# Gated linear attention and mLSTM on one core: two of eight score products joined, the weight sum of mLSTM taken from summed tiles, and the gate product split over two groups of rows

## The chip, the cores and the metric

The kernel runs on one core of one Trainium2 chip. The metric is the device time of one execution in microseconds (us): the median of several runs. The engines named below are PE (the matrix engine, with its weight loads shown apart as PEld), DVE (the vector engine), ACT (the scalar engine), POOL (GpSimd) and SP, which issues transfers. SBUF is the on-chip memory with 128 partitions, PSUM the memory that PE writes its products to, in banks of 512 float32 columns.

## The reference, cut to what matters

One layer of a decoder on 512 tokens and 16 meta tokens. Its token mixing has three branches; the change touches two of them, each with four heads.

```python
def gla_chunk_step(S, xs):                 # gated linear attention (GLA)
    q, k, v, g = xs
    G = jnp.cumsum(g, axis=2)
    causal = jnp.tril(jnp.ones((C, C), bool))
    diff = G[:, :, :, None, :] - G[:, :, None, :, :]
    decay = jnp.exp(jnp.where(causal[None, None, :, :, None], diff, -jnp.inf))
    A = jnp.einsum("bhtk,bhtsk,bhsk->bhts", q, decay, k)
    o = jnp.einsum("bhtk,bhkv->bhtv", q * jnp.exp(G), S) + jnp.einsum("bhts,bhsv->bhtv", A, v)
...
    g = jax.nn.log_sigmoid((a_lr @ p["w_gla_a2"] + p["b_gla_a"]).astype(jnp.float32)) / GLA_TAU
...
def mlstm_chunk_step(carry, xs):
    P = jnp.exp(D - m[..., None]) * jnp.einsum("bhtk,bhsk->bhts", q, k)
    num = w_inter[..., None] * jnp.einsum("bhtk,bhkv->bhtv", q, Cs) + jnp.einsum("bhts,bhsv->bhtv", P, v)
    den = w_inter * jnp.einsum("bhtk,bhk->bht", q, ns) + jnp.sum(P, axis=-1)
    h = num / jnp.maximum(jnp.abs(den), jnp.exp(-m))[..., None]
```

## The kernel before, in words

All engines run programs written out by hand, in a fixed order; they wait for each other by semaphores. PE is given one long list of work. Its bulk are the projections (`gemm`), each of them three products of a high and a low part of weights and activations in the type `fp32r`, a shortened float32 (PE's rows print it as `f32` too). Their weights stream in by transfers (`wraw`) and are split by POOL into `whi` and `wlo`, four chunks ahead at most. Results go to two PSUM tiles `GP`, used in turn; the attention work between them uses the four banks of `PA`, called `bank(0)` to `bank(3)`. A product with plain float32 operands is shown in the trace as two records, one behind the other.

**GLA.** Inside a tile of 128 tokens the decay between a query and an earlier key can't be one factor, since it would overflow. So the 128 x 128 weights of a tile are put together from seven levels, `LEVELS = [64, 32, 16, 8, 4, 2, 1]`, and the diagonal. On a level with blocks of B tokens, queries in the odd blocks meet keys in the even block just before. For each level DVE writes the two halves of the exponents into `E` (`lv_write`), ACT takes the exponential (`level`), DVE multiplies the 256 queries into `QL` and the 256 keys into `KL` (`lv_mul`), PE takes four products of 64 columns (`level`, L2129), and DVE copies the wanted entries into `AT` under a mask (`lv_select`, L1451). The diagonal is `level(h, 7)`: the plain product of `kh` and `qh`, four times 128 x 128 (L2132), of which `lv_select` takes the diagonal (L1454). Between the levels PE does pieces of the projections of the next head: level 6 and the diagonal stand between two halves of `gv..A` (L1845; in the last head a gate, L1830). Behind the second half PE waits for the last selection, for `KHt` (L1459) and for `km` (`twice`, L1186), and transposes them (L2183, L2185).

**The gate product.** `gemm("gg..")` (L1850) multiplies the 16 rows of `w_gla_a2`, put into rows 32 to 47 of the otherwise zero `a2`, with `small`, 128 rows of 528 columns, in two halves of 264 columns that go to two banks. Head 0's stands before the level loop, those of heads 1 to 3 between levels 0 and 1 of the head before.

**mLSTM.** For four blocks j of keys, `AT[:, j, :]` holds the weights of all queries from `FROM[j]` on (`FROM = [0, 112, 240, 368]`), so 512, 400, 272 and 144 columns, and `ATt` the 16 last queries' weights for the last 16 keys. `weights_of(h, j)` on DVE makes them from the scores and from `Wd` (ACT, `decay`). PE's `recalled` sums over the blocks in PSUM (L2239, L2240): twice with the values, into banks 0 and 1, and a third time with `ones`, into bank 3, which is the sum of the weights. `denominator` on DVE reads it. DVE's own order behind `weights_of(h, 3)` is: the convolutions of the next head (`conv`, `conv_mul`), with `km` at their end, then `denominator(h)` and `head_sums(h)`, for which PE's `squares` (L2147) in the next head waits.

Of the kernel before, what the change touches and what calls it, by code (L numbers as in the profile page):

```python
# [24 lines left out]
D = 1024  # L25
SEQ = 512
# [265 lines left out]
def build(nc, a, line, scratch, rows, out):  # L292
# [3 lines left out]
    with ctx:  # L296
# [6 lines left out]
        def region(offset, specs):  # L303
# [67 lines left out]
        AO = YO + 2 * KT * SEQ * 4  # L371
        (sgate, gtmp, vb, qh, kh, vh, vm, AT, ATm, sqo, rso, on, km) = region(AO, [
            ("sgate", [P, 2, SEQ], FP32), ("gtmp", [P, 2, SEQ], FP32), ("vb", [P, D], FP32),
            ("qh", [P, 2, SEQ], FP32), ("kh", [P, 2, ALL], FP32), ("vh", [P, 2, QT, DV], FP32),
            ("vm", [P, 2, DV], FP32), ("AT", [P, QT, SEQ], FP32), ("ATm", [P, SEQ], FP32),
            ("sqo", [P, 2, SEQ], FP32), ("rso", [P, SEQ], FP32), ("on", [P, 2, SEQ], FP32), ("km", [P, 2, P], FP32)])
# [7 lines left out]

        (zc, cv, sgc, lf_, bcum_, M_, uT, uTt, fbias_, um_, Mb, Md, Wd, Mt, Wt, ATt, later_t, ones16) = region(BO, [
            ("zc", [P, ALL + 3], FP32), ("cv", [P, ALL], FP32), ("sgc", [P, ALL], FP32), ("lf", [P, ALL], FP32),
# [3 lines left out]
            ("Mt", [2 * META, META], FP32), ("Wt", [2 * META, META], FP32), ("ATt", [P, META], FP32),  # L390
            ("later_t", [2 * META, META], FP32), ("ones16", [P, P], FP32)])
        later = ATm
        states, keysT = AT[:, :, P:P + DV], AT[:, :, P + DV:SEQ]

# [233 lines left out]
        def _(act):  # L628
# [538 lines left out]
        def _(dve):  # L1167
# [201 lines left out]
            dve.wait_ge(gla_c, 1)  # L1369
            dve.wait_ge(ld_a, 32)  # L1370

# [11 lines left out]
            def q_in(h):  # L1383
                ts(qh[:, h % 2, :], ready(f"gq{h}")[:, 0:SEQ], cc("gq", h), DK ** -0.5, ALU.add, ALU.mult).then_inc(gfree[tl[f"gq{h}"].slot], 1)

# [25 lines left out]
            def lv_write(h, l):  # L1411

                B = LEVELS[l]
                lo_, up = parts(G[:, h % 2, META:ALL], B)
                N = SEQ // (2 * B)
                mid = lo_[:, :, B - 1:B].broadcast_to([P, N, B])
                k = len(LEVELS) * h + l
                if k:
                    dve.wait_ge(lv_qk, k)
                dve.wait_ge(G_ok, h + 1)  # L1420
                tt(E[:, 0:SEQ // 2].rearrange("p (n b) -> p n b", b=B), up, mid, ALU.subtract)
                tt(E[:, SEQ // 2:SEQ].rearrange("p (n b) -> p n b", b=B), mid, lo_, ALU.subtract).then_inc(lv_w, 1)

            def lv_mul(h, l):
                B = LEVELS[l]
                k = len(LEVELS) * h + l
                dve.wait_ge(lv_e, k + 1)
                if k >= 2:
                    dve.wait_ge(lv_ps, 8 * ((k - 2) // 7) + (k - 2) % 7 + 1)
                _, uq = parts(qh[:, h % 2, :], B)  # L1430
                lk, _ = parts(kh[:, h % 2, META:ALL], B)
                lo_, _ = parts(KL[:, k % 2, :], B)
                tt(QL[:, k % 2, :].rearrange("p (n b) -> p n b", b=B), uq, E[:, 0:SEQ // 2].rearrange("p (n b) -> p n b", b=B), ALU.mult)
                if k:
                    dve.wait_ge(lv_qk, k)
                tt(lo_, lk, E[:, SEQ // 2:SEQ].rearrange("p (n b) -> p n b", b=B), ALU.mult).then_inc(lv_qk, 1)

            def lv_select(h, l):
                k = 8 * h + l
                dve.wait_ge(lv_ps, k + 1)  # L1440
                if k == 8 * h and h:
                    dve.wait_ge(av_ps, h)
                if k:
                    dve.wait_ge(lv_sel, k)
                if l < len(LEVELS):
                    B = LEVELS[l]
                    n_ = P - B
                    o_ = AT[0:n_, :, 0:P].rearrange("p t (n two b) -> p t n two b", two=2, b=B)[:, :, :, 1, :]
                    m_ = lm[0:n_, l, :].rearrange("p (n b) -> p n b", b=B).unsqueeze(1).broadcast_to([n_, QT, 64 // B, B])
                    d_ = bank(k % 4)[0:n_, 0:QT * 64].rearrange("p (t n b) -> p t n b", t=QT, b=B)  # L1450
                    nc.vector.copy_predicated(o_, m_.bitcast(U32), d_).then_inc(lv_sel, 1)  # L1451
                else:
                    m_ = ident[:, :].unsqueeze(1).broadcast_to([P, QT, P])
                    nc.vector.copy_predicated(AT[:, :, 0:P], m_.bitcast(U32),  # L1454
                                              bank(k % 4).rearrange("p (t n) -> p t n", t=QT)).then_inc(lv_sel, 1)

            def off(h):
# [3 lines left out]
                twice(km[:, h % 2, 0:2 * META], KHt[:, 0:META], km_ok)  # L1461
                tt(QQ[:, :], QQ[:, :], qh[:, h % 2, :], ALU.mult).then_inc(od_q, 1)
                if h + 1 < HEADS:
# [100 lines left out]
            def gate_rows_of(m):  # L1564

                if m == 0:
                    nc.vector.memset(zc[:, 0:3], 0.0).then_inc(zpad, 1)
                    nc.vector.memset(M_[GR, :], 1.0).then_inc(M_one, 1)
                    nc.vector.tensor_copy(bcum, small[96:96 + HEADS, :]).then_inc(ms_d, 1)
# [3 lines left out]
                if m == 1:  # L1573
                    dve.wait_ge(fl_ok, 1)
                    seq(ts(bcum, bcum, 0.0, None, ALU.min))
                    seq(tt(lf, bcum, lf, ALU.subtract))
                    dve.wait_ge(M_one, 1)
                    seq(nc.vector.tensor_tensor_scan(bcum, M, lf, 0.0, ALU.mult, ALU.add))
# [9 lines left out]
                if m == 4:  # L1588
                    nc.vector.memset(ATt[:, :], 0.0)
                    nc.vector.memset(later[:, :], 0.0)  # L1590
                    nc.vector.memset(ones16[:, :], 0.0).then_inc(ml_c, 1)
                    dve.wait_ge(ml_c, 1)
                    nc.vector.memset(ones16[0:META, :], 1.0).then_inc(ml_c, 1)
                if m == 5:
# [57 lines left out]
            def weights_of(h, j):  # L1652
# [29 lines left out]
            for q in range(2):  # L1682
                conv(0, q)
                conv_mul(0, q)
            dve.wait_ge(ml_c, 3)
            dve.wait_ge(ld_v, 16)
            for part in range(3):
                values("mv", 0, part)
            for h in range(HEADS):
# [8 lines left out]
                weights_of(h, 2)  # L1698
                weights_of(h, 3)
                if more:  # L1700
                    conv(h + 1, 0)
# [96 lines left out]
        def _(pe):  # L1798
# [9 lines left out]
            def gemm(name, part=None):  # L1808
# [304 lines left out]

            pe.wait_ge(ld_a, 32)

            def level(h, l):
                k = 8 * h + l
                if l < len(LEVELS):
                    pe.wait_ge(lv_qk, 7 * h + l + 1)
                if k >= 4:  # L2120
                    pe.wait_ge(lv_sel, k - 3)
# [3 lines left out]
                for i in range(QT):  # L2125
                    if l < len(LEVELS):
                        b = (7 * h + l) % 2
# [20 lines left out]

            for nm in ("gq0", "gk0", "gg0", "gv0A", "gv0B", "gv0M"):
                gemm(nm)  # L2150
            for h in range(HEADS):
# [24 lines left out]
                level(h, 6)  # L2176
                level(h, 7)
                nxt("gvA", 1)
# [63 lines left out]
            for h in range(HEADS):  # L2242
# [8 lines left out]
                if h == 0:  # L2251
                    pe.wait_ge(ml_c, 3)
                nxt("mq", 0)
# [145 lines left out]
```

## Time and profile before

| | us |
|---|---|
| median of 3 runs | 1278.88 |
| lowest, highest | 1278.63, 1279.53 |
| the profiled execution, whole | 1279.91 |
| its span, first to last instruction | 1278.2 |
| PE busy in it | 1270.2 |
| DVE, ACT, POOL busy in it | 613.8, 393.9, 774.5 |
| granted TensorE clock | 1.0 throughout |

The trace shows GLA from about 347 to 570 us of the span, mLSTM from about 665 to 800 us. PE is busy for 99% of the span. A merged row of the timeline gives the first start and the busy time of several records of one line. The records of PE overlap, since the modelled end of a matmul includes its way through the array; how long a group holds the engine is therefore read from one start to the next start, not from the busy column.

### The profile page before, as it was taken

Reading aid. Unit: us, or ns where it says so; the run is one execution under the profiler, and the core shown is the slowest. Engines: PE = TensorE matmul, PEld = TensorE weight load, DVE = VectorE, ACT = ScalarE, POOL = GpSimd, SP = SyncE. Lnnn points to the kernel's source line nnn. Section 1 sums busy time; section 2 is a strip of 40 time slices with the busy share of each in tenths; the row PEclk is TensorE's granted clock in tenths of the full one; section 3 lists DMA queues with packets and bytes.
Section 4 is the critical chain, followed back from the end, with each engine's and each line's share of the span. In section 5 each row is a group of like instructions: output and inputs, shape, how many; then the busy total and the mean of one; then the engine's idle time right before and its main releaser. Section 6 shows DMA issues by size and latency. Waiting matters only on the chain.

```text
span 1278.2 us, 17629 instructions
## 1 busy us (share of the span) xinstructions
PE 1270.2 (99%) x6665; PEld 1043.6 (82%) x6668; DVE 613.8 (48%) x1090; ACT 393.9 (31%) x810; POOL 774.5 (61%) x919
## 2 busy tenths in 40 slices
PE   9999999999999999999999999999999999999998
PEld 8866887676899899888898887787888888888886
DVE  4248788652266877825445562242611112333434
ACT  4243565543013324234023333311501101221322
POOL 8737430034763753758774446786677667788882
PEclk9999999999999999999999999999999999999999
DMA  7755200222322312222442323533233333222321
GB/s 186 221 173 166 75 17 26 66 68 79 95 74 60 83 50 67 74 76 83 114 111 72 85 83 99 172 108 99 67 100 98 99 85 113 99 84 98 100 83 66
DMA packets 168444, 120.59 MB, mean 94 GB/s; under 512 B 12393, under 2 KB 146639, under 8 KB 168360
## 3 DMA queue, kind: packets, MB, share of 16 engines
q1 hardware_dynamic: 161654, 108.32, 29.1%
q10 hardware_dynamic: 6706, 11.15, 2.6%
q8 instruction: 53, 0.87, 0.3%
q14 instruction: 31, 0.25, 0.1%
HBM read 115.20 MB, written 9.62 MB: 98 GB/s over the span
## 4 chain that ended last, share of the span: by engine, by line
PE 99%; ACT 0%; DVE 0%; issue 0%; DVEq 0%; ACTq 0%
PE GP L1830 45%; PE GP L1865 9%; PE PA L1865 9%; PE GP L1845 7%; PE GP L1827 7%; PE PA L2029 3%; PE GP L2091 3%; PE PA L2239 2%; PE PA L2129 2%; PE PA L2066 1%; PE GP L2312 1%; PE GP L1910 1%; PE PA L1999 1%; PE PA L2231 1%; PE PA L2030 1%; PE GP L1837 1%
## 5 line engine op out<-in xcount | busy, mean ns | idle before, releaser
L623 POOL TENSOR_TENSOR wlo<-wraw,whi 128x256 fp32r<-128x256 f32 x712 | 565.9, 826 | 14.8
L619 POOL TENSOR_SCALAR whi<-wraw 128x1024 fp32r<-128x1024 f32 x178 | 201.6, 1132 | 464.5 <-PE GP L1830 228.7
L1830 PE MATMUL GP<-xh,whi 128*128 128x512 f32 x352 | 145.5, 413 | 0.0
L1830 PE MATMUL GP<-xh,wlo 128*128 128x512 f32 x352 | 139.1, 395 | 0.0
L1830 PE MATMUL GP<-xl,whi 128*128 128x512 f32 x352 | 138.9, 394 | 0.0
L1772 DVE TENSOR_TENSOR ul<-U,uh 128x512 fp32r<-128x512 f32 x64 | 65.4, 1057 | 109.4 <-ACT uh L1146 109.4
L1830 PE MATMUL GP<-nl,whi 128*128 128x512 f32 x240 | 95.1, 396 | 0.0
L1830 PE MATMUL GP<-nh,wlo 128*128 128x512 f32 x240 | 95.1, 396 | 0.0
L1830 PE MATMUL GP<-nh,whi 128*128 128x512 f32 x240 | 95.1, 396 | 0.0
L1776 DVE SCALAR_TENSOR_TENSOR U<-GP,rrow 128x512 f32<-128x512 f32 x32 | 22.1, 691 | 141.7 <-PE GP L1830 140.3
L1830 PEld LDWEIGHTS GP<-xh,whi 128*128 128x128 f32 x352 | 66.2, 188 | 16.3 <-issue 2.0
L1830 PEld LDWEIGHTS GP<-xh,wlo 128*128 128x128 f32 x352 | 66.1, 188 | 15.3
L1830 PEld LDWEIGHTS GP<-xl,whi 128*128 128x128 f32 x352 | 66.4, 189 | 14.6 <-issue 1.0
L1146 ACT ACTIVATE uh<-U 128x512 fp32r<-128x512 f32 x64 | 37.3, 628 | 128.9 <-PE PA L1865 70.3
L1830 PE MATMUL GP<-yh,whi 128*128 128x512 f32 x192 | 76.3, 398 | 0.0
L1830 PE MATMUL GP<-yl,whi 128*128 128x512 f32 x192 | 76.1, 396 | 0.0
L1830 PE MATMUL GP<-yh,wlo 128*128 128x512 f32 x192 | 76.1, 396 | 0.0
L1845 PE MATMUL GP<-whi,xh 128*128 128x256 f32 x256 | 73.8, 288 | 0.0
L1845 PE MATMUL GP<-wlo,xh 128*128 128x256 f32 x256 | 71.9, 281 | 0.0
L1845 PE MATMUL GP<-whi,xl 128*128 128x256 f32 x256 | 71.6, 280 | 0.0
L1150 ACT ACTIVATE U<-U 128x512 f32<-128x512 f32 x32 | 20.2, 632 | 152.8 <-DVE U L1776 152.8
L1830 PEld LDWEIGHTS GP<-nh,wlo 128*128 128x128 f32 x240 | 45.2, 188 | 11.0
(414 smaller groups left out, 2796.6 us busy)
## 6 DMA issues: line engine op xcount, KB each, us to landing
wraw<-in_w_in SPq DMA_DIRECT2D x75, 512.0 KB, 3.8
wraw<-in_w_up SPq DMA_DIRECT2D x32, 512.0 KB, 4.0
wraw<-in_w_down SPq DMA_DIRECT2D x32, 512.0 KB, 3.5
line_rows<-bias_line SPq DMA_DIRECT2D x8, 655.0 KB, 5.0
table<-line_rows SPq DMA_DIRECT2D x4, 1024.0 KB, 5.4
wraw<-in_w_br_dsa SPq DMA_DIRECT2D x8, 512.0 KB, 4.1
wraw<-in_w_br_gla SPq DMA_DIRECT2D x8, 512.0 KB, 3.9
wraw<-in_w_br_ml SPq DMA_DIRECT2D x8, 512.0 KB, 4.1
```

Source lines behind the costliest of these rows:

```text
L619: nc.gpsimd.tensor_scalar(hi, src, 1.0, 1.0, ALU.mult, ALU.mult).then_inc(hi_done, 1)
L623: part = nc.gpsimd.tensor_tensor(lo[:, at:to], src[:, at:to], hi[:, at:to].bitcast(FP32), ALU.subtract)
L1146: nc.scalar.activation(uh[:, k % 4, :], U[:, k % FT, :], ACT.Copy).then_inc(uh_ok, 1)
L1772: tt(ul[:, k % 4, :], U[:, k % FT, :], uh[:, k % 4, :].bitcast(FP32), ALU.subtract).then_inc(ul_ok, 1)
L1827: ins = mm(ps[0:t.m, b * SEQ:b * SEQ + HALF], wt[:, s0, w], hx[:, k, b * HALF:(b + 1) * HALF], start=st, stop=sp_)
L1830: ins = mm(ps[0:t.m, 0:SEQ], wt[:, s0, w], av, start=st, stop=sp_)
L1845: ins = mm(o_, at_[:, k, tok], wt[:, s0:s0 + 2, k * P:(k + 1) * P], start=(k == 0 and p_ == 0), stop=(k == KT - 1 and p_ == 2))
L1865: ins = mm(accumulators(name, hf, i), av[:, i * P:(i + 1) * P], wt[:, c["hl"], k * SEQ:(k + 1) * SEQ], start=(n == 0 and k == 0 and p_ == ...
L2029: mm(bank(v % 2)[0:r, 0:w], qlat[:, h, TILE_AT[i]:TILE_AT[i + 1]], kvT[:, 0:w], start=True, stop=False)
L2091: ins = mm(pairs_of(o_, g), kvn[:, j, :], pairs_of(PT[:, g % 2, j, :], g), start=(j == 0), stop=(j == i))
L2129: ins = mm(bank(k % 4)[0:n_, i * 64:(i + 1) * 64], KL[:, b, i * P:i * P + n_], QL[:, b, i * 64:(i + 1) * 64], start=True, stop=True)
L2239: mm(b[:, FROM[j]:SEQ], lhs(j), AT[:, j, 0:SEQ - FROM[j]], start=(j == 0), stop=False)
```

## The change

Three things are done, in both engines' programs.

1. **GLA, levels 6 and 7 joined.** `qh` of GLA becomes `qg`, four tiles of 192 columns: 128 queries, and behind them the 64 odd queries times their decay on level 6. For blocks of one token the factor of the keys is exp(0) = 1, so that the level takes the plain keys, as the diagonal does. `lv_write`, ACT's exponential and `lv_mul` therefore drop the half of the keys on level 6, and PE takes four products of 192 columns with `kh` as weights, into banks 2 and 3, two tiles each. DVE then selects in two pieces for the level and two for the diagonal. All readers of the queries in GLA (`lv_mul`, `off`) now read tiles that are 192 columns apart.
2. **mLSTM, weights summed.** DVE adds the four blocks' weights into `Wd[:, 0, :]` (`weight_sums`, behind `weights_of(h, 3)`), and PE takes only `AT[:, 0, 0:112]` and the sum's 400 other columns with `ones`. `ones16` and its two fills are gone.
3. **Gate product in two row groups.** `w_gla_a2` is loaded twice, into rows 32 to 47 and 0 to 15 of `a2`; DVE copies the second half of rows 32 to 63 of `small` to rows 0 to 31; the two halves of the product use rows 32 to 63 and 0 to 31. PE's wait for the loads moves behind `gq0` and `gk0`.

```diff
@@ ACT
-            act.dma_start(a2[32:32 + META, :], a["w_gla_a2"][0]).then_inc(ld_a, 16)
+            for r in (2 * META, 0):
+                act.dma_start(a2[r:r + META, :], a["w_gla_a2"][0]).then_inc(ld_a, 16)
...
-                nc.scalar.activation(E[:, :], E[:, :], ACT.Exp, scale=1.0 / 16.0).then_inc(lv_e, 1)
+                n_ = SEQ // 2 if LEVELS[l] == 1 else SEQ
+                nc.scalar.activation(E[:, 0:n_], E[:, 0:n_], ACT.Exp, scale=1.0 / 16.0).then_inc(lv_e, 1)
@@ DVE
+            nc.vector.tensor_copy(small[0:2 * META, HALF:ALL], small[2 * META:4 * META, HALF:ALL]).then_inc(gla_c, 1)
-            dve.wait_ge(ld_a, 32)
+            dve.wait_ge(ld_a, 48)
...
+                uq = qg[:, h % 2, :, 0:P].rearrange("p t (n two b) -> p t n two b", two=2, b=B)[:, :, :, 1, :]
+                if B == 1:
+                    tt(qg[:, h % 2, :, P:P + P // 2], uq.rearrange("p t n b -> p t (n b)"),
+                       E[:, 0:SEQ // 2].rearrange("p (t n) -> p t n", t=QT), ALU.mult).then_inc(lv_qk, 1)
+                    return
...
-                    m_ = ident[:, :].unsqueeze(1).broadcast_to([P, QT, P])
-                    nc.vector.copy_predicated(AT[:, :, 0:P], m_.bitcast(U32),
-                                              bank(k % 4).rearrange("p (t n) -> p t n", t=QT)).then_inc(lv_sel, 1)
+                    single = l < len(LEVELS)
+                    m_ = lm[:, l, :] if single else ident[:, :]
+                    n_ = P // 2 if single else P
+                    for hf in range(2):
+                        o_ = AT[:, 2 * hf:2 * hf + 2, 1:P:2] if single else AT[:, 2 * hf:2 * hf + 2, 0:P]
+                        d_ = bank(2 + hf)[:, 0:3 * P].rearrange("p (t n) -> p t n", t=2)
+                        d_ = d_[:, :, P:P + n_] if single else d_[:, :, 0:P]
+                        ins = nc.vector.copy_predicated(o_, m_.unsqueeze(1).broadcast_to([P, 2, n_]).bitcast(U32), d_)
+                        if hf == 0:
+                            seq(ins)
+                    ins.then_inc(lv_sel, 1)
...
+            def weight_sums(h):
+                dve.wait_ge(at_ok, 5 * h + 5)
+                t = Wd[:, 0, :]
+                seq(tt(t[:, FROM[1]:SEQ], AT[:, 0, FROM[1]:SEQ], AT[:, 1, 0:SEQ - FROM[1]], ALU.add))
+                for j in (2, 3):
+                    seq(tt(t[:, FROM[j]:SEQ], t[:, FROM[j]:SEQ], AT[:, j, 0:SEQ - FROM[j]], ALU.add))
+                t = t[0:META, SEQ - META:SEQ]
+                tt(t, t, ATt[0:META, :], ALU.add).then_inc(sum_w, 1)
@@ PE
-                        ins = mm(ps[:, b * SEQ:b * SEQ + HALF], a2[:, h * DK:(h + 1) * DK], small[:, b * HALF:(b + 1) * HALF],
+                        r = slice(2 * META * (1 - b), 2 * META * (2 - b))
+                        ins = mm(ps[:, b * SEQ:b * SEQ + HALF], a2[r, h * DK:(h + 1) * DK], small[r, b * HALF:(b + 1) * HALF],
...
-                        ins = mm(bank(k % 4)[:, i * P:(i + 1) * P], kh[:, h % 2, META + i * P:META + (i + 1) * P],
-                                 qh[:, h % 2, i * P:(i + 1) * P], start=True, stop=True)
-                ins.then_inc(lv_ps, 1)
+                        w = P + P // 2
+                        ins = mm(bank(2 + i // 2)[:, i % 2 * w:(i % 2 + 1) * w], kh[:, h % 2, META + i * P:META + (i + 1) * P],
+                                 qg[:, h % 2, i, :], start=True, stop=True)
+                ins.then_inc(lv_ps, 1 + (l == len(LEVELS) - 1))
...
-                recalled(bank(3), lambda j: ones[:, :], ones16[:, :]).then_inc(av_ps, 1)
+                mm(bank(3)[:, 0:FROM[1]], ones[:, :], AT[:, 0, 0:FROM[1]], start=True, stop=True)
+                pe.wait_ge(sum_w, h + 1)
+                mm(bank(3)[:, FROM[1]:SEQ], ones[:, :], Wd[:, 0, FROM[1]:SEQ], start=True, stop=True).then_inc(av_ps, 1)
```

The built programs show what stands in a row. PE at the end of the levels of head 0, before: level 6 (`QL,KL`) and the diagonal (`qh,kh`) between the two halves of the values' projection.

```order
1370 L1845 MATMUL GP<-whi,xl 128x256
1371 L2129 MATMUL PA<-QL,KL 127x64 x4
1372 L2132 MATMUL PA<-qh,kh 128x128 x4
1373 L1845 MATMUL GP<-whi,xh 128x256
1374 L1845 MATMUL GP<-wlo,xh 128x256
```

The same place in the changed kernel.

```order
1370 L1874 MATMUL GP<-whi,xl 128x256
1371 L2163 MATMUL PA<-qg,kh 128x192 x4
1372 L1874 MATMUL GP<-whi,xh 128x256
1373 L1874 MATMUL GP<-wlo,xh 128x256
```

One group of four has taken the place of two, and nothing else moved. DVE at the same place, before, from the last multiplications of a level to `km`:

```order
437 L1433 TENSOR_TENSOR QL<-qh,E 128x256
438 L1436 TENSOR_TENSOR KL<-kh,E 128x256
439 L1451 COPY_PREDICATED AT<-lm,PA 126x4x32x2
440 L1451 COPY_PREDICATED AT<-lm,PA 127x4x64
441 L1454 COPY_PREDICATED AT<-ident,PA 128x4x128
442 L1459 TENSOR_TENSOR KHt<-KHt,kh 128x400
443 L1186 COPY km<-KHt 128x32
```

And in the changed kernel:

```order
437 L1440 TENSOR_TENSOR qg<-qg,E 128x4x64
438 L1463 COPY_PREDICATED AT<-lm,PA 126x4x32x2
439 L1472 COPY_PREDICATED AT<-lm,PA 128x2x64 x2
440 L1472 COPY_PREDICATED AT<-ident,PA 128x2x128 x2
441 L1479 TENSOR_TENSOR KHt<-KHt,kh 128x400
442 L1189 COPY km<-KHt 128x32
```

The multiplication of the keys is gone, and four selections stand where two stood, ahead of `KHt` and `km`. PE in mLSTM, head 0, behind the products with the values, before:

```order
2691 L2240 MATMUL PA<-ATt,vm 128x16
2692 L2239 MATMUL PA<-AT,ones 128x512
2693 L2239 MATMUL PA<-AT,ones 128x400
2694 L2239 MATMUL PA<-AT,ones 128x272
2695 L2239 MATMUL PA<-AT,ones 128x144
2696 L2240 MATMUL PA<-ATt,ones 128x16
2697 L1845 MATMUL GP<-whi,xh 128x256
```

And in the changed kernel, where the second of the two waits for DVE's sums:

```order
2687 L2274 MATMUL PA<-ATt,vm 128x16
2688 L2304 MATMUL PA<-AT,ones 128x112
2689 L2306 MATMUL PA<-Wd,ones 128x400
2690 L1874 MATMUL GP<-whi,xh 128x256
```

Two products of 512 columns together have taken the place of five with 1344.

## Rows read from the trace of the kernel before

**Rows 1.** The page: busy us and share of each engine, and the chain that ended last.

```profile
PE 1270.2 (99%) x6665; PEld 1043.6 (82%) x6668; DVE 613.8 (48%) x1090; ACT 393.9 (31%) x810; POOL 774.5 (61%) x919
...
PE 99%; ACT 0%; DVE 0%; issue 0%; DVEq 0%; ACTq 0%
...
L619 POOL TENSOR_SCALAR whi<-wraw 128x1024 fp32r<-128x1024 f32 x178 | 201.6, 1132 | 464.5 <-PE GP L1830 228.7
```

**Rows 2.** Timeline of PE, GLA head 0: start us, busy us, line, records.

```profile
398.38 0.28 PE L1845 MATMUL GP<-whi,xl 128*128 128x256 f32 x1
398.50 0.99 PE L2129 MATMUL PA<-QL,KL 128*127 128x64 f32 x8
399.33 1.11 PE L2132 MATMUL PA<-qh,kh 128*128 128x128 f32 x8
400.19 0.37 PE L1845 MATMUL GP<-whi,xh 128*128 128x256 f32 x1
400.40 0.28 PE L1845 MATMUL GP<-wlo,xh 128*128 128x256 f32 x1
```

**Rows 3.** PE's groups by form: records, busy us in all, mean ns of one record.

```profile
L2239 PE MATMUL PA<-AT,vh 128*128 128x400 f32 x16 | 6.7, 499 | 0.0
L2239 PE MATMUL PA<-AT,vh 128*128 128x272 f32 x16 | 5.0, 392 | 0.0
L2239 PE MATMUL PA<-AT,vh 128*128 128x144 f32 x16 | 3.3, 286 | 0.0
```

**Rows 4.** Timeline of PE, mLSTM head 0; the group merges the four widths.

```profile
681.13 2.48 PE L2239 MATMUL PA<-AT,ones 128*128 128x512 f32 x8
683.45 0.29 PE L2240 MATMUL PA<-ATt,ones 128*128 128x16 f32 x2
683.59 0.37 PE L1845 MATMUL GP<-whi,xh 128*128 128x256 f32 x1
```

**Rows 5.** Timeline: head 0's gate product, `kh` on DVE; the gate product in a loop.

```profile
352.93 1.05 PE L1850 MATMUL GP<-small,a 128*128 128x264 f32 x4
353.95 0.38 PE L1845 MATMUL GP<-whi,xh 128*128 128x256 f32 x1
...
353.13 0.77 DVE L1387 TENSOR_SCALAR kh<-GP,col 128x528 f32<-128x528 f32 x1 [4.96 <-PE GP L1827]
...
429.39 1.16 PE L1850 MATMUL GP<-small,a 128*128 128x264 f32 x4
430.38 0.81 PE L2129 MATMUL PA<-QL,KL 128*96 128x64 f32 x8
```

**Rows 6.** Timeline of PE: two products of 64 rows each, between ordinary ones.

```profile
70.23 0.40 PE L1830 MATMUL GP<-cql,whi 128*128 128x512 f32 x1
70.47 0.39 PE L1830 MATMUL GP<-cqh,wlo 128*128 128x512 f32 x1
70.79 0.70 PE L1999 MATMUL PA<-kn,qi 64*128 64x256 f32 x4
71.42 0.50 PE L1830 MATMUL GP<-cqh,whi 128*128 128x512 f32 x1
71.76 0.39 PE L1830 MATMUL GP<-cql,whi 128*128 128x512 f32 x1
```

**Rows 7.** Timeline of DVE, GLA head 0, to `km`; then PE's transposition of it.

```profile
393.59 0.43 DVE L1451 COPY_PREDICATED AT<-lm,PA 124x256 f32<-124x256 uint32 x1
...
399.53 0.73 DVE L1451 COPY_PREDICATED AT<-lm,PA 127x256 f32<-127x256 uint32 x1 [2.98 <-PE PA L2129]
400.48 0.74 DVE L1454 COPY_PREDICATED AT<-ident,PA 128x512 f32<-128x512 uint32 x1 [0.22 <-PE PA L2132]
401.11 0.55 DVE L1459 TENSOR_TENSOR KHt<-KHt,kh 128x400 f32<-128x400 f32 x1
401.70 0.18 DVE L1186 COPY km<-KHt 128x32 f32<-128x32 f32 x1
...
403.12 0.27 PE L2183 MATMUL PA<-ident,km 128*128 128x128 f32 x1
```

**Rows 8.** Timeline: DVE's work on levels, PE's level 2 in head 3, POOL's splitting.

```profile
385.71 0.41 DVE L1436 TENSOR_TENSOR KL<-kh,E 128x256 f32<-128x256 f32 x1
386.16 0.43 DVE L1421 TENSOR_TENSOR E<-G 128x256 f32<-128x256 f32 x1
...
387.96 1.26 DVE L1436 TENSOR_TENSOR KL<-kh,E 128x256 f32<-128x256 f32 x1
...
531.16 0.96 DVE L1436 TENSOR_TENSOR KL<-kh,E 128x256 f32<-128x256 f32 x1
...
532.62 0.91 PE L2129 MATMUL PA<-QL,KL 128*112 128x64 f32 x8
...
396.24 2.83 POOL L623 TENSOR_TENSOR wlo<-wraw,whi 128x256 fp32r<-128x256 f32 x4
```

**Rows 9.** Timeline of DVE, mLSTM heads 0 and 1: last weights, `km`, denominator.

```profile
670.98 0.15 DVE L1660 TENSOR_TENSOR ATt<-PA,Wt 32x16 f32<-32x16 f32 x1
...
717.36 0.18 DVE L1186 COPY km<-kh 128x32 f32<-128x32 f32 x1
719.25 0.69 DVE L1666 TENSOR_TENSOR gtmp<-PA,lf 128x512 f32<-128x512 f32 x1 [1.72 <-PE PA L2240]
```

More of the change, by code:

```diff
@@ L1383, in q_in @@
             def q_in(h):
-                ts(qh[:, h % 2, :], ready(f"gq{h}")[:, 0:SEQ], cc("gq", h), DK ** -0.5, ALU.add, ALU.mult).then_inc(gfree[tl[f"gq{h}"].slot], 1)
+                ts(qg[:, h % 2, :, 0:P], ready(f"gq{h}")[:, 0:SEQ].rearrange("p (t n) -> p t n", t=QT), cc("gq", h), DK ** -0.5, ALU.add, ALU.mult).then_inc(gfree[tl[f"gq{h}"].slot], 1)
             def k_in(h):
@@ L1429, in lv_mul @@
                     dve.wait_ge(lv_ps, 8 * ((k - 2) // 7) + (k - 2) % 7 + 1)
-                _, uq = parts(qh[:, h % 2, :], B)
+                tiles = lambda t: t.rearrange("p (t n b) -> p t n b", t=QT, b=B)
+                uq = qg[:, h % 2, :, 0:P].rearrange("p t (n two b) -> p t n two b", two=2, b=B)[:, :, :, 1, :]
+                if B == 1:
+                    tt(qg[:, h % 2, :, P:P + P // 2], uq.rearrange("p t n b -> p t (n b)"),
+                       E[:, 0:SEQ // 2].rearrange("p (t n) -> p t n", t=QT), ALU.mult).then_inc(lv_qk, 1)
+                    return
                 lk, _ = parts(kh[:, h % 2, META:ALL], B)
                 lo_, _ = parts(KL[:, k % 2, :], B)
-                tt(QL[:, k % 2, :].rearrange("p (n b) -> p n b", b=B), uq, E[:, 0:SEQ // 2].rearrange("p (n b) -> p n b", b=B), ALU.mult)
+                tt(tiles(QL[:, k % 2, :]), uq, tiles(E[:, 0:SEQ // 2]), ALU.mult)
                 if k:
@@ L1444, in lv_select @@
                     dve.wait_ge(lv_sel, k)
-                if l < len(LEVELS):
+                if l < len(LEVELS) - 1:
                     B = LEVELS[l]
@@ L1461, in off @@
                 twice(km[:, h % 2, 0:2 * META], KHt[:, 0:META], km_ok)
-                tt(QQ[:, :], QQ[:, :], qh[:, h % 2, :], ALU.mult).then_inc(od_q, 1)
+                qq = QQ[:, :].rearrange("p (t n) -> p t n", t=QT)
+                tt(qq, qq, qg[:, h % 2, :, 0:P], ALU.mult).then_inc(od_q, 1)
                 if h + 1 < HEADS:
@@ L1589, in gate_rows_of @@
                     nc.vector.memset(ATt[:, :], 0.0)
-                    nc.vector.memset(later[:, :], 0.0)
-                    nc.vector.memset(ones16[:, :], 0.0).then_inc(ml_c, 1)
+                    nc.vector.memset(later[:, :], 0.0).then_inc(ml_c, 1)
                     dve.wait_ge(ml_c, 1)
-                    nc.vector.memset(ones16[0:META, :], 1.0).then_inc(ml_c, 1)
                 if m == 5:
@@ L1684, in _ @@
                 conv_mul(0, q)
-            dve.wait_ge(ml_c, 3)
+            dve.wait_ge(ml_c, 2)
             dve.wait_ge(ld_v, 16)
@@ L1699, in _ @@
                 weights_of(h, 3)
+                weight_sums(h)
                 if more:
@@ L2112, in _ @@
                 gemm(f"yb{m}")
-            pe.wait_ge(ld_a, 32)
             def level(h, l):
                 k = 8 * h + l
-                if l < len(LEVELS):
-                    pe.wait_ge(lv_qk, 7 * h + l + 1)
-                if k >= 4:
+                pe.wait_ge(lv_qk, 7 * h + l + 1)
+                if l == len(LEVELS) - 1:
+                    pe.wait_ge(lv_sel, k - 2)
+                elif k >= 4:
                     pe.wait_ge(lv_sel, k - 3)
@@ L2147, in squares @@
                 mm(bank(2), ones[:, :], sqo[:, 0, :], start=True, stop=True).then_inc(av_ss, 1)
-            for nm in ("gq0", "gk0", "gg0", "gv0A", "gv0B", "gv0M"):
+            gemm("gq0")
+            gemm("gk0")
+            pe.wait_ge(ld_a, 48)
+            pe.wait_ge(gla_c, 2)
+            for nm in ("gg0", "gv0A", "gv0B", "gv0M"):
                 gemm(nm)
@@ L2176, in _ @@
                 level(h, 6)
-                level(h, 7)
                 nxt("gvA", 1)
@@ L2251, in _ @@
                 if h == 0:
-                    pe.wait_ge(ml_c, 3)
+                    pe.wait_ge(ml_c, 2)
                 nxt("mq", 0)
```

21 lines of the change are left out of this document (11 added, 10 removed).

## The prediction, made before the changed kernel ran

> **What bounds the kernel now.** I read the page first. PE is busy for 1270.2 of 1278.2 us, and the chain that ended last is PE for 99% of the span [rows 1]. So a microsecond that PE no longer needs is a microsecond of the result, unless it turns into a wait; and time on DVE, ACT or POOL costs nothing until PE waits for it. POOL, which splits PE's weights, stood idle for 464.5 us ahead of its first step, mostly waiting for PE [rows 1]: weights can come faster. The question is thus twofold: what do the removed products hold PE for, and which of the edits on DVE come due.
>
> A product's price has to be read from start to start. Plain float32 records of 144, 272 and 400 columns have means of 286, 392 and 499 ns [rows 3]: 106 or 107 ns more for 128 columns more, 0.83 ns a column, the rest being the way through the array, which overlaps. A record holds PE for 0.83 ns a column if nothing else binds: 128 columns make 0.107 us.
>
> **GLA, the joined product.** Level 6 starts at 398.50, the diagonal at 399.33, the next projection at 400.19 [rows 2]. That last one lasts 0.37 instead of 0.28 and its successor starts 0.21 behind it, where such records otherwise stand 0.12 apart (398.38 to 398.50): it began 0.09 late, at 400.28. So the two groups hold PE for 1.78 us. The diagonal's eight records of 128 columns take 0.86, the 0.107 each of the column rate. Level 6's eight records take 0.83, or 0.104 each, though 64 columns would need 0.053: something else binds there, and what each record also has is a weight load of 127 columns. The new product has eight records of 192 columns, 0.160 each, which is longer than what bound level 6: 1.28 us, with the late start of the next record gone. Saved: 0.50 a head, 2.0 us in four.
> The Trainium skill (TensorE: Matmul & The Clock Gate, "Back-to-back issue gap") gives about 60 cycles for any matmul of up to 64 columns. Taken alone that rule speaks against this edit: level 6 would cost no more than its columns, 8 x 0.053 = 0.43 us, and joining it to the diagonal would save about nothing. The trace's 0.104 us a record contradicts it here and fits the same page's other rule ("LDWEIGHTS (loading the stationary operand)"): a load takes its columns / 1.2 ns, 107 ns for 128.
>
> **What DVE must do behind it.** The end of the product starts a chain: selections, `KHt`, `km`, and PE's transposition of `km`. Before, the diagonal's selection began at 400.48, 0.20 after the product's end, and `km` ended at 401.88; PE took it at 403.12, its weight load 0.11 earlier, so the chain had 1.1 us in hand [rows 7]. Now the product ends at 398.50 + 1.28 = 399.78 and the first selection can start at 399.98. Of a selection the trace shows 0.43 us for 256 elements in runs of four and 0.74 for 512 [rows 7], that is 0.12 and 1.2 ns an element; level 6's single elements took 0.73 for 256, twice that rate. The new pieces have 128 single elements or 256 in a row: 0.43 each, and 0.45 from start to start where each waits for the one before, as `KL` and the next `E` do at 385.71 and 386.16 [rows 8]. Three of those, then 0.32 to `KHt` (which starts 0.11 before its forerunner's end, as at 401.11), then 0.59 and 0.18: 399.98 + 1.35 + 0.32 + 0.77 = 402.42. PE now asks at 403.01 - 0.50 = 402.51. The cover shrinks from 1.1 us to 0.1. I book 0.05 a head for it, 0.2 in all; the other end is 0.74 for every piece, as the finest selection shows: 1.2 later, 1.1 us of wait a head.
> The strided queries make the level's multiplication at worst as much slower as single elements made a selection, 0.3. The tightest place is level 2 of head 3: `KL` ends at 532.12 [rows 8] and PE's level starts at 532.62, its weights 0.11 earlier [rows 8]. At worst some 0.5 us in that one head; I take none, since only whole tiles are 192 apart and the runs inside are as long as before. The dropped half of level 6 on DVE and ACT gives time back off the path.
>
> **mLSTM, the sum of the weights.** From 681.13 to 683.59 PE is held 2.46 us; both that start and the next show the same 0.09 of lateness [rows 4]. Now: 2 records of 400 columns at 0.333, and 2 of 112, for which I take the 0.107 of a full weight load: 0.88 us. Saved 1.58 a head, 6.3 us in four; between 6.2 (the next start still 0.09 late only once) and 6.6 (112 columns at their own 0.093, late start gone).
> DVE adds 400, 272, 144 and 16 columns. A tensor-tensor operation of 400 took 0.55 [rows 7] and the small one 0.15 [rows 9]; with 0.40 and 0.27 between them that is 1.4 us, at the contended rate of [rows 8] (1.26 against 0.41) up to 4. The weights are complete at 671.13 in head 0 and PE reaches the sum at 681.13: ten microseconds of cover. Behind the additions stand the next head's convolutions, `km` and the denominator: in head 1 `km` ends at 717.54 and DVE then idles 1.72 us for PE [rows 9]. The 1.4 us fill that gap, and PE comes 1.6 earlier, so the denominator is some 1.3 us late against PE. Its first reader on PE is the sum of squares, with the two other value products and half a projection before it; nothing waits.
>
> **The gate product.** Four records of 264 columns, 0.22 each, 0.88. In the loop the first starts 0.10 late (busy 1.16 against 1.05 in head 0), since the 64-column tiles of level 0 must leave the array first: 429.39 + 0.10 + 0.88 = 430.37, and level 1 starts at 430.38 [rows 5]. The trace has products in halves of the rows: 70.79. The slot of the record before it ends at 70.47 + 0.24 = 70.71, and the next ordinary one starts late by 0.10 (0.50 against 0.39), at 71.52: 0.82 us. Four records of 256 columns would stream for 0.85 one after another and for 0.43 two by two. So they ran two by two, and the change of form cost 0.39, about 0.20 on each side [rows 6]. For the gate: 0.10 ahead, which is already paid, 0.44, and 0.20 behind: 0.74 against 0.98, saving 0.24 in each of three loops, 0.7 us. In head 0 nothing: the next product waits for `kh` (ended 353.90) until 353.95 anyway, and the gate's records were over at 353.81 [rows 5]. Bounds: 1.3 saved without the switch behind, 0.8 lost if the groups run in turn and the switch is paid.
> The Trainium skill (TensorE: Matmul & The Clock Gate, "Measured speedup vs the span model") counts one matmul's time and 4 ns a tile for packed products; by that alone it would be 1.3 us. The trace agrees on the overlap, but its 0.39 us of switching is not in that model.
>
> **The sum.** 2.0 + 6.3 + 0.7 - 0.2 = 8.8 us. The profiled execution took 1279.91 (span 1278.2 and 1.7 around it), 1.0 above the median; against it this gives 1271.1, against the median 1278.88 it gives **1270.1**.
>
> **Rivals.**
> - Row groups that don't pay: the 32-row tiles run in turn, or the switch costs more than in [rows 6]. The gate then loses 0.8: 1271.6. For it: no row has 32-row groups. Against: the 64-row pair. 0.14.
> - The selections come due: 0.74 a piece, 1.1 us in four heads, 4.4 instead of 0.2: 1274.3. For it: the cover is only 0.1. Against: 0.43 for 256 elements. 0.06.
> - Level 6 cost only its columns, by the issue floor: the joined product saves nothing, 1272.1. Against: 0.104 a record. 0.03. The rule is the skill's, weighed above.
> - It doesn't do what it says: PE needs less, but the weights' stream sets the pace, and the savings come back as waits: 1278.9. Against: POOL's 464.5 idle us. 0.03.
> - Slower: the four selections collide with POOL's splitting, at 1.26 us each as in [rows 8]: 0.83 x 4 - 0.1 = 3.2 us of wait a head, 12.8 in all, less 9.0: 1282.7. It outweighs the gain from 2.3 a head on. Against: POOL's splitting there ends at 399.07, before the selections [rows 8]. 0.02.
>
> **How the numbers follow.** The forecast has 0.72. What a measurement can tell from no change is 0.2%, 2.6 us; the first three rivals are beyond it on the fast side: faster 0.72 + 0.14 + 0.06 + 0.03 = 0.95, same 0.03, slower 0.02. The range takes the gate's bounds, the mLSTM bound, 0.3 us a head of wait for `km` and the 0.9 us by which runs differ: 1269.0 to 1272.6.
>
> **What would show it.** The 192-column group's start to the next start 1.3 us; the sum with `ones` 0.9 us; the gate 0.75 in the loop, its records in pairs with the same start; `km` ending just before PE's transposition, with no idle PE or up to 0.1. Wrong would be: idle PE ahead of L2183's counterpart, gate records one behind another, or level products of head 3 that wait for `KL`.

## The result, and the profile after

| | before | after |
|---|---|---|
| median, us | 1278.76 (4 runs, 1278.52 to 1279.53) | 1270.57 (4 runs, 1270.31 to 1271.16) |
| the profiled execution, whole | 1279.91 | 1270.31 |
| its span | 1278.2 | 1268.6 |
| PE busy in it | 1270.2 | 1260.5 |

The ratio is 0.9935, with a 95% interval of 0.9921 to 0.9950: 8.2 us faster, where 8.8 were forecast. All medians below are over executions at the full granted clock; left out are one of `sums_only` (1779.46 us at 0.65, its profiled one, so that no row of it is used) and one of the kernel before beside it (2096.71 us at 0.56). The first lines of the page of after, busy us and share of each engine and the chain that ended last, answer to [rows 1]: PE is still the whole of the chain, with less to do, and DVE has 7 us more.

```profile
PE 1260.5 (99%) x6612; PEld 1034.7 (82%) x6612; DVE 621.0 (49%) x1105; ACT 392.9 (31%) x810; POOL 775.0 (61%) x919
...
PE 99%; DVE 0%; ACT 0%; issue 0%; DVEq 0%; ACTq 0%
```

**The joined product**, against [rows 2]. The timeline of PE in the changed kernel, head 0 of GLA (start, busy, line, operation, records), from the product to the transposition of `km`:

```profile
396.77 0.28 PE L1874 MATMUL GP<-whi,xl 128*128 128x256 f32 x1
396.89 1.46 PE L2163 MATMUL PA<-qg,kh 128*128 128x192 f32 x8
398.06 0.41 PE L1874 MATMUL GP<-whi,xh 128*128 128x256 f32 x1
398.31 0.28 PE L1874 MATMUL GP<-wlo,xh 128*128 128x256 f32 x1
...
400.91 0.28 PE L1874 MATMUL GP<-whi,xl 128*128 128x256 f32 x1
401.17 0.30 PE L2217 MATMUL PA<-ident,km 128*128 128x128 f32 x1
401.31 0.49 PE L2219 MATMUL PA<-ident,KHt 128*128 128x128 f32 x3
```

The product starts at 396.89; the next record starts at 398.06 and is 0.13 late (0.41 instead of 0.28), so PE is held for 1.30 us, where it was 1.78. Then comes what is new: the transposition of `km` starts 0.26 us behind its forerunner, which otherwise takes 0.12, and is itself 0.03 late: 0.17 us of wait. From the level's start to the transposition's it is 4.28 us against 4.62 before.

The saving rests on level 6 having been bound by its weight loads and not by its 64 columns. The kernel before shows this itself, since its levels have the same 64 columns and different numbers of weight columns. Three of them by form (records, busy us in all, mean ns of one):

```profile
L2129 PE MATMUL PA<-QL,KL 128*127 128x64 f32 x32 | 4.0, 267 | 0.0
L2129 PE MATMUL PA<-QL,KL 128*96 128x64 f32 x32 | 3.3, 247 | 0.0
L2129 PE MATMUL PA<-QL,KL 128*64 128x64 f32 x32 | 2.7, 228 | 0.0
```

From record to record the trace has a median of 0.058 us with 64 weight columns, 0.085 with 96, 0.098 with 112 and 0.111 with 127: the spacing follows the weight columns.

DVE at the same place, against [rows 7]:

```profile
398.39 0.92 DVE L1472 COPY_PREDICATED AT<-lm,PA 128x128 f32<-128x128 uint32 x2 [3.47 <-PE PA L2163]
399.42 0.93 DVE L1472 COPY_PREDICATED AT<-ident,PA 128x256 f32<-128x256 uint32 x2
400.25 0.56 DVE L1479 TENSOR_TENSOR KHt<-KHt,kh 128x400 f32<-128x400 f32 x1
400.84 0.18 DVE L1189 COPY km<-KHt 128x32 f32<-128x32 f32 x1
```

The four selections take 1.86 us up to `KHt`, and `km` ends at 401.02, just when PE's next slot came free (400.91 and 0.12). By the prediction's reading PE's weight load should have begun 0.11 earlier.

**The sum of the weights**, against [rows 4], PE in head 0 of mLSTM:

```profile
677.74 0.45 PE L2304 MATMUL PA<-AT,ones 128*128 128x112 f32 x2
678.03 0.85 PE L2306 MATMUL PA<-Wd,ones 128*128 128x400 f32 x2
678.41 0.59 PE L1874 MATMUL GP<-whi,xh 128*128 128x256 f32 x1
678.83 0.28 PE L1874 MATMUL GP<-wlo,xh 128*128 128x256 f32 x1
```

The busy column of the third row tells that it started in truth 0.31 later than drawn, at 678.72. With the 0.09 at the start taken off as before, the two products hold PE for 0.89 us instead of 2.46.

**The gate product**, against [rows 5], PE in the loop of head 0:

```profile
426.86 0.68 PE L2159 MATMUL PA<-QL,KL 128*64 128x64 f32 x8
427.46 0.71 PE L1880 MATMUL GP<-small,a 32*128 32x264 f32 x4
428.11 0.89 PE L2159 MATMUL PA<-QL,KL 128*96 128x64 f32 x8
```

From 427.46 to 428.11, and 0.08 that the next group is late (0.89 against 0.81): 0.73 us instead of 0.99. The busy time of the four records together, 0.71, is less than the 0.88 that they need one after another. In the trace they start at 427.46, 427.47, 427.79 and 427.80: in two pairs, as the prediction had asked for as its sign.

Set side by side, operation by operation, the two traces also differ by 1.3 us in their first 8 us, where the programs are the same; the last section comes to that. From there on the profiled executions differ by 8.3 us, as the medians do. Where they come from, by the distance between the same operations in both traces, and by kernels with one part each (next section):

| part | forecast | in the traces | alone, by medians |
|---|---|---|---|
| joined product, less its wait | 2.0 - 0.2 | 1.3 (four times 0.5 - 0.17) | 1.2 |
| sum of the weights | 6.3 | 6.2 (1.55 a head) | 6.5 |
| gate product | 0.7 | 0.76 (three loops) | 0.7 |
| together | 8.8 | 8.3 | 8.4 |

### The profile page after: what moved, and what is told of

Read it like the earlier page. It is cut to its first block, busy times and chain, and to the rows that moved or that the text cites. A ratio compares the mean times of both kernels' runs of the same rounds, so it can differ in the third digit from the quotient of the medians.

```text
span 1268.6 us, 17537 instructions
## 1 busy us (share of the span) xinstructions
PE 1260.5 (99%) x6612; PEld 1034.7 (82%) x6612; DVE 621.0 (49%) x1105; ACT 392.9 (31%) x810; POOL 775.0 (61%) x919
## 4 chain that ended last, share of the span: by engine, by line
PE 99%; DVE 0%; ACT 0%; issue 0%; DVEq 0%; ACTq 0%
PE GP L1859 46%; PE GP L1895 9%; PE PA L1895 9%; PE GP L1874 7%; PE GP L1856 7%; PE PA L2059 3%; PE GP L2121 3%; PE PA L2159 1%; PE PA L2096 1%; PE PA L2273 1%; PE GP L2348 1%; PE GP L1940 1%; PE PA L2029 1%; PE PA L2265 1%; PE PA L2060 1%; PE GP L1866 1%
```

## The experiments

Each kernel was run beside the kernel before on the same chip. The column "alone, by medians" above is from the first three.

### One part at a time

Each of these is the kernel before with one part of the diff shown above, with what belongs to it.

`sums_only`, part 2:

> The kernel before with part 2 alone (the weights summed on DVE). Theory: PE is the only bound and the additions have ten microseconds of cover, so each head gives back what the product with ones no longer holds PE for. From the trace of after, 1.54 us a head: 6.2 us, 1272.6. Rival: the additions delay the convolutions and the denominator until PE waits for them; then under 5 us are left, and idle PE shows in mLSTM.

Measured: 1272.59 (four executions) against 1279.12 (20), 6.5 us, ratio 0.9948 (0.9934 to 0.9962). The theory holds, the rival (under 5 us) doesn't.

`gla_only`, part 1:

> The kernel before with part 1 alone (level 6 and the diagonal joined). Theory: 0.5 us a head from PE, of which a wait of 0.15 to 0.2 us for km takes a part: 1.3 to 1.4 us in all, 1277.4. Rival 1: no wait, the late transposition is only a way the trace draws it: 2.0 us, 1276.8. Rival 2: level 6 cost only its columns: no gain, 1278.8.

Measured: 1277.93 against 1279.12, 1.2 us, ratio 0.9990 (0.9981 to 0.9999). Nearest to the theory. The interval alone would not exclude 2.0, but in its trace the same operations stand as in the changed kernel: each head gains 0.5 us at the projection behind the product and gives back 0.17 to 0.25 at the transposition.

`gate_only`, part 3:

> The kernel before with part 3 alone (the gate product in two groups of 32 rows). Theory: 0.25 us in each of three loops and nothing in head 0: 0.75 us, 1278.0, and the gate's four records start in two pairs. Rival 1: packed products without a price for the change of form: 0.44 a loop, 1.3 to 1.7 us, 1277.3. Rival 2: the groups run in turn: up to 0.8 us slower, 1279.6.

Measured: 1278.41 against 1279.12, 0.7 us, ratio 0.9992 (0.9983 to 1.0001). By time alone that can't be told from nothing; the trace decides. PE in its loop of head 0:

```profile
427.70 0.68 PE L2131 MATMUL PA<-QL,KL 128*64 128x64 f32 x8
428.31 0.71 PE L1853 MATMUL GP<-small,a 32*128 32x264 f32 x4
428.95 0.89 PE L2131 MATMUL PA<-QL,KL 128*96 128x64 f32 x8
```

0.64 and 0.08 here too, in each of three loops. The three parts give 8.4 us when each is alone and 8.2 together: within the scatter they don't touch each other.

### What the gate's 0.73 us are made of

`one_group`, the changed kernel with one line more:

```diff
-                        r = slice(2 * META * (1 - b), 2 * META * (2 - b))
+                        r = slice(2 * META, 4 * META)
```

> The changed kernel with both halves of the gate product on the same group of 32 rows (32 to 63). Theory: the gain of the gate is the overlap of two groups and its price the change of form. Without the overlap the four records run in turn, 0.22 us each, and the price stays: 0.44 us more in three loops and 0.2 to 0.3 in head 0, where it runs into the wait for kh: 1.5 to 1.7 us slower than the changed kernel, 1272.2, and slower there than the product over 128 rows. Rival: the gain came from fewer rows, not from the overlap: no change, 1270.6.

Measured: 1271.98 against 1278.88, ratio 0.9946 (0.9934 to 0.9959): 6.9 us of the 8.2 are left, 1.3 are lost, a little less than the theory's 1.5 to 1.7. PE in its loop of head 0:

```profile
428.19 0.68 PE L2159 MATMUL PA<-QL,KL 128*64 128x64 f32 x8
428.80 1.15 PE L1880 MATMUL GP<-small,a 32*128 32x264 f32 x4
429.88 0.89 PE L2159 MATMUL PA<-QL,KL 128*96 128x64 f32 x8
```

1.08 and 0.08 late: 1.16 us, against 0.73 with two groups and 0.99 over all 128 rows. So the overlap is worth 0.43, the time of one of the two products. Of the 1.16 us the four records need 0.88; the other 0.28 are the changes between the forms of the array, 0.10 ahead, which the kernel before paid too, and 0.17 to 0.18 behind (1.16 less 0.99). Without the overlap, 32 rows are slower than 128.

### Whether the late transposition waits for `km`

Two ways to take away what makes it late. `keys_first` makes `KHt` and `km` ahead of the last four selections:

```diff
@@ DVE, in the loop over heads
-                for l in range(5, 8):
+                lv_select(h, 5)
+                keys_out(h)
+                for l in range(6, 8):
                     lv_select(h, l)
                 off(h)
@@ PE
-                pe.wait_ge(lv_sel, 8 * h + 8)
+                pe.wait_ge(lv_sel, 8 * h + 6)
                 pe.wait_ge(od_q, 6 * h + 1)
...
+                pe.wait_ge(lv_sel, 8 * h + 8)
                 pe.wait_ge(od_ev, h + 1)
```

(`keys_out` holds the first two operations of `off`.)

> The changed kernel with one thing more: on DVE, KHt and km are made ahead of the last four selections instead of behind them, and PE's transpositions wait only for the selections of level 5 and before; the wait for all selections moves to PE's next own product. Theory: the 0.15 to 0.2 us by which the transposition of km was late in each head were a wait for km at the end of the chain of selections; they go, 0.6 to 0.8 us in all, 1269.9. Rival: they belong to the 192-column form (a late weight load), and stay: 1270.6, with the transposition as late as before though km is ready.

`two_selects` leaves the order and takes one selection over both banks in the place of two:

```diff
-                    for hf in range(2):
...
+                    o_ = (AT[:, :, 1:P:2] if single else AT[:, :, 0:P]).rearrange("p (a t) n -> p a t n", a=2)
+                    d_ = PA[1][:, :].rearrange("p (a b) -> p a b", a=2)[:, :, 0:3 * P].rearrange("p a (t n) -> p a t n", t=2)
+                    d_ = d_[:, :, :, P:P + n_] if single else d_[:, :, :, 0:P]
+                    m_ = m_.unsqueeze(1).unsqueeze(1).broadcast_to([P, 2, 2, n_])
+                    nc.vector.copy_predicated(o_, m_.bitcast(U32), d_).then_inc(lv_sel, 1)
```

> The changed kernel with two selections in the place of four: one for level 6 and one for the diagonal, each over both banks. Theory (the chain of selections made km late): two of 0.74 us take some 0.4 us less than four of 0.46, so that km is ready 0.2 us before PE asks: 0.6 to 0.8 us faster than the changed kernel, 1269.9. Rival (the lateness is PE's own): no change, 1270.6.

`keys_first_two` has both:

> Both at once: KHt and km ahead of the selections, and two selections instead of four. Theory: either of the two removes the whole wait, so both give the same as one, 0.6 to 0.8 us faster than the changed kernel, 1269.9. Rival: each removes a part or another wait for the selections is left behind the first: faster than either alone by 0.2 us or more.

PE in `two_selects`, the last projection record and the transposition, then DVE there:

```profile
401.31 0.28 PE L1871 MATMUL GP<-whi,xl 128*128 128x256 f32 x1
401.43 0.27 PE L2214 MATMUL PA<-ident,km 128*128 128x128 f32 x1
...
398.80 0.73 DVE L1472 COPY_PREDICATED AT<-lm,PA 128x256 f32<-128x256 uint32 x1 [3.46 <-PE PA L2160]
399.63 0.75 DVE L1472 COPY_PREDICATED AT<-ident,PA 128x512 f32<-128x512 uint32 x1
400.27 0.56 DVE L1476 TENSOR_TENSOR KHt<-KHt,kh 128x400 f32<-128x400 f32 x1
400.87 0.18 DVE L1189 COPY km<-KHt 128x32 f32<-128x32 f32 x1
```

The selections take 1.47 us up to `KHt` instead of 1.86, `km` ends at 401.05, and PE takes it 0.12 behind its forerunner and not late. In `keys_first` the transposition stands the same, 0.12 behind:

```profile
401.19 0.28 PE L1878 MATMUL GP<-whi,xl 128*128 128x256 f32 x1
401.31 0.27 PE L2221 MATMUL PA<-ident,km 128*128 128x128 f32 x1
```

So it was a wait for `km`. Counted between the same operations of two traces, each of the two edits gives 0.14 to 0.23 us a head, 0.7 in all, and both together no more than one. In time, for `keys_first`, `two_selects` and `keys_first_two`: ratios of 0.9929 (0.9916 to 0.9942), 0.9930 (0.9917 to 0.9944) and 0.9930 (0.9918 to 0.9943), medians 1270.52, 1269.95 and 1269.82. `two_selects` was run once more beside the changed kernel.

> The changed kernel as it is, beside the next two on the same chip. All theories: 1270.6, or 8.2 to 8.4 us less than the kernel before.

> Two selections for four once more, now beside the changed kernel. Theory: the wait for km of 0.17 us a head is gone, 0.6 to 0.8 us less than the changed kernel. Rival: the difference of the first comparison was scatter, under 0.3 us.

Measured: 1270.51 (1269.98 to 1271.63) and 1270.08 (1269.69 to 1270.67) against 1279.02, ratios 0.9933 and 0.9930. The difference of 0.4 us lies within the scatter of either, between the theory's 0.6 and the rival's 0.3, and decides nothing. The traces do: counted from the first transposition of the inputs to the end of the span, which leaves the start-up out (last section), the two traces of the changed kernel are 8.3 and 8.4 us shorter than the kernel before, and those of `keys_first`, `keys_first_two` and `two_selects` (twice) 9.1 to 9.2. None of the three forms is faster than another.

### How much cover the additions have

`sums_long` repeats the first addition on DVE nine times, `sums_mid` five times:

```diff
-                seq(tt(t[:, FROM[1]:SEQ], AT[:, 0, FROM[1]:SEQ], AT[:, 1, 0:SEQ - FROM[1]], ALU.add))
+                for _ in range(9):
+                    seq(tt(t[:, FROM[1]:SEQ], AT[:, 0, FROM[1]:SEQ], AT[:, 1, 0:SEQ - FROM[1]], ALU.add))
```

> The changed kernel with DVE's first addition of 400 columns done nine times instead of once (the same result each time): some 4.3 us more on DVE in each head of mLSTM, ahead of the next head's convolutions. Theory: ten microseconds of cover for the sum and seven for what stands behind it, so no change, 1270.6 within 0.3. Rival: something behind the additions (km, the value tiles, the denominator) is nearer to PE than the rows of before let me count; then PE waits show in mLSTM and the time rises by up to 4 us a head.

Measured: 1279.27 (1278.49 to 1279.74) against 1278.88, ratio 1.0001 (0.9992 to 1.0009). The whole gain of the change is gone: 8.7 us by the medians. By the distance between the same operations in the traces it is 8.5: 2.4, 2.8 and 2.8 us in the three heads that have a next one, and 0.5 in the last. The rival was right. Who made PE wait, by the view of waits of PE (us in all, times, longest) in `sums_long`:

```profile
PE GP L1875 <- ACT zc L980: 3.6, 3, 1.2
PE GP L1857 <- DVE vh L1380: 1.6, 2, 1.0
PE GP L1860 <- DVE vh L1380: 1.0, 1, 1.0
...
PE PA L2307 <- DVE Wd L1689: 0.2, 1, 0.2
```

Hardly the sum itself (`Wd`, once, 0.2, in the last head). Two things behind the additions are nearer to PE. `zc` is ACT's evacuation of the next head's key projection: it waits for the convolution on DVE that still reads the buffer, and PE needs its PSUM tile for the next value projection. `vh` is DVE's evacuation of the second of the next head's three value products, last but one in DVE's queue of the head; its tile is the one that PE's projection behind the third needs. DVE in the changed kernel shows how near they are, additions first, then the end of the queue:

```profile
667.77 0.58 DVE L1684 TENSOR_TENSOR Wd<-AT 128x400 f32<-128x400 f32 x1
668.38 1.62 DVE L1686 TENSOR_TENSOR Wd<-Wd,AT 128x272 f32<-128x272 f32 x2
670.03 0.59 DVE L1688 TENSOR_TENSOR Wd<-Wd,ATt 16x16 f32<-16x16 f32 x1
...
682.02 0.69 DVE L1702 SCALAR_TENSOR_TENSOR sqo<-gtmp,sqo 128x512 f32<-128x512 f32 x1
684.58 0.69 DVE L1380 TENSOR_TENSOR vh<-GP,vb 128x512 f32<-128x512 f32 x1 [1.86 <-PE GP L1874]
```

The additions took 2.85 us, from 667.77 to 670.62, twice what I had worked out from rows without POOL beside them. DVE idles 1.86 us ahead of `vh` in this head and 1.46 in the two after it, and `vh` then ends at 685.27, about 1.0 us before PE is through with the third value product (the next projection starts at 686.22). So the cover is 2.4 to 2.8 us, not ten. Before the change the same `vh` had 3.8 us in each head, the 2.86 of idle time below and the same 1.0 behind it; the change has used 1.0 to 1.4 us of that.

```profile
689.52 0.69 DVE L1376 TENSOR_TENSOR vh<-GP,vb 128x512 f32<-128x512 f32 x1 [2.86 <-PE GP L1845]
```

ACT's `zc` ended at 675.06 with PE asking at 678.6: 3.6 us, the next in line.

> The changed kernel with DVE's first addition of 400 columns five times instead of once. Nine times cost 2 us a head in spite of the ten microseconds before the sum is wanted: PE waited for the evacuation of the next head's key projection, which on ACT follows the convolution that stands behind the additions on DVE. In the changed kernel that evacuation ended 3.6 us before PE asked for its PSUM tile. Theory: four more additions end the chain some 2 us later than in the changed kernel (they run at 0.5 to 0.8 us each, but the other additions then fall outside POOL's splitting): inside the 3.6 us, no change, 1270.6 within 0.3. Rival: the price of additions on DVE has no such cover and grows in proportion, half of the nine-fold one: 1 us a head, 1274.9.

I had taken the 3.6 us for the first limit; the 2.4 to 2.8 come before it. Measured: 1271.69 (1270.68 to 1271.79) against 1279.02, ratio 0.9939 (0.9927 to 0.9951), beside 1270.51 for the changed kernel. So neither the theory's 0.3 nor the rival's 4.4: 1.2 us by the medians, 0.7 by the traces, nothing of it in head 0 and 0.37 in each of the next two. DVE in `sums_mid`, head 1, and PE's next projection:

```profile
718.54 0.69 DVE L1703 SCALAR_TENSOR_TENSOR sqo<-gtmp,sqo 128x512 f32<-128x512 f32 x1
719.15 0.68 DVE L1380 TENSOR_TENSOR vh<-GP,vb 128x512 f32<-128x512 f32 x1
...
719.69 0.28 PE L1867 MATMUL GP<-wlo,xm 128*32 128x256 f32 x1
720.09 0.49 PE L1857 MATMUL GP<-xh,whi 128*128 128x264 f32 x2
```

DVE no longer idles ahead of `vh`, which ends at 719.83, and PE's projection starts 0.40 behind a record that holds it for 0.12: the cover is just used up, by a chain that ends 2.5 us later. PE starts 0.26 us behind the end of `vh`, in `sums_long` 0.25, so that much of the cover can't be used. With nine additions both waits are open, that for `zc` and that for `vh`, 0.6 to 1.2 us each. What of the medians' 1.2 us isn't in this trace stays open; the scatter of single runs is of that size.

## Why the prediction was right, point by point

- **PE is the only bound, and a product's price is read from start to start.** Right. The removed time came out of the total in full: 8.3 us in the traces, 8.2 in the medians.
- **The sum of the weights, 6.3 us.** Right within 0.1: 0.89 us held against the 0.88 worked out from the column rate.
- **The joined product, 2.0 us.** Right: 1.30 us against the predicted 1.28, 0.48 to 0.50 saved a head. That level 6 was bound by its weight loads and not by its 64 columns is what the saving rests on; the spacing of the levels' records (0.058 to 0.111 us for 64 to 127 weight columns) shows it, and `gla_only` shows by its trace that something was saved. So the Trainium skill's issue floor (TensorE: Matmul & The Clock Gate, "Back-to-back issue gap") was not what level 6 cost, as the 0.104 us a record had said.
- **The wait for `km`, 0.05 a head.** This is the term that was mis-sized: 0.17 a head, 0.7 in all instead of 0.2, which is nearly all of what lies between the forecast 8.8 us and the 8.3 of the traces. The sum had the selections 0.45 apart. They are 0.45 long, as forecast, but start at 398.39, 398.87, 399.42 and 399.90: 0.48 apart within a group and 0.55 between the groups, which makes 1.86 us to `KHt` instead of 1.67. The chain has 6 links, and at a margin of 0.1 us an error of 0.2 decides. Of its own signs the prediction allowed up to 0.1 of idle PE here; there was more. `keys_first` and `two_selects` show that it is this wait.
- **The gate, 0.74 against 0.98 a loop.** Right: 0.73 against 0.99, and nothing in head 0, where PE now waits 0.2 us for `kh`. Both ingredients were tested: the overlap (0.43) and the price of the change of form (0.17 more than before, 0.28 with the side that was paid already). The Trainium skill's model (same page, "Measured speedup vs the span model"), one product's time and 4 ns a tile, has the overlap and not this price; by that model alone the gate would have saved an estimated 1.3 us.
- **The additions on DVE cost nothing.** Right in the result, wrong in the step, and so right by luck. I had counted ten microseconds from the weights to the product, 1.4 us for the additions, and for what stands behind them only `km` and the denominator. The additions took 2.85, inside the bound of 4 given for the contended rate. What PE waits for first behind them is the evacuation of the second value product, `vh`, which the prediction doesn't name: its cover was 3.8 us in the kernel before and is 2.4 to 2.8 now, and four more additions use it up.

## What to carry to other kernels

Before work is moved to an idle engine, find for everything queued behind it on that engine who waits for it next, evacuations of PSUM tiles above all; the distance to the moved result's own reader says little. A product of few columns can cost its weight load, as level 6 did (0.111 us a record for 64 columns and 127 weight columns), and joining it to another with the same weights is then worth more than its columns. Splitting a product over groups of rows pays only while what is overlapped is more than the changes of form, here 0.10 us ahead and 0.18 behind, and 0.39 together for the pair of [rows 6].

## What the runs showed of the hardware that I had not expected

The start of the program doesn't take the same time in each execution: in the twelve profiled ones at the full clock the first transposition of the inputs starts between 8.4 and 10.0 us of the span, whatever the kernel. PE begins with a row of like products of 128 columns. The timeline of twenty of them in the changed kernel, and then in another execution of the same kernel (`after_again`):

```profile
2.68 3.26 PE L1916 MATMUL PA<-ones 128*128 128x128 f32 x20
5.78 1.88 PE L1923 MATMUL GP<-grow,ones 128*128 128x512 f32 x4
```

```profile
2.68 4.47 PE L1916 MATMUL PA<-ones 128*128 128x128 f32 x20
6.95 1.28 PE L1923 MATMUL GP<-grow,ones 128*128 128x512 f32 x2
```

The same twenty records take 3.1 or 4.3 us to the next product. In the first trace they start 0.213 us apart up to 4.5 us of the span and 0.112 from there on; in the second all are 0.213 apart. That is PE at the lower and then at the higher of its two clock levels, 1.2 and 2.4 GHz: the view of the clock prints 1.00 for these stretches, but the entries of the granted clock in the two traces begin only at 4.5 and at 7.5 us, in the first just where the records turn. PE had been busy since 1.24 us in both. Over the twelve executions the first entry lies between 4.1 and 7.5 us; what sets the moment these runs don't tell.

The kernel before had its first entry at 7.2 us, so that the profiled executions differ by 9.6 us and the medians by 8.2. Counted from the first transposition of the inputs, at about 9 us, the two traces of the changed kernel differ by 0.1 us, where their spans differ by 1.3, and the two of `two_selects`, which turned within 0.1 us of each other, by less than 0.1. The fastest and the slowest run of one kernel lie 0.9 to 1.7 us apart; that most of this comes from the start is argued and not shown, since the other runs have no trace. It is a reason to seek half a microsecond in traces, from behind the start, and not in a median.

DVE's operations with both operands in SBUF slowed beside POOL's splitting more than I had allowed: additions of 272 and 144 columns together took 1.62 us in the changed kernel, from 668.38 on, while POOL made `wlo` from 667.78 to 671.63. In `sums_long`, where POOL had ended at 671.88, they took 0.78. Not every one is slowed: the first addition of 400 columns, from 667.77 on, took 0.58 with POOL beside it.

```profile
674.77 0.78 DVE L1687 TENSOR_TENSOR Wd<-Wd,AT 128x272 f32<-128x272 f32 x2
```
